# Seven sub-products for eight in one feed-forward layer of a two-layer diffusion backbone

## What is computed

```
def swiglu(t, w_in, w_out):
    gate, up = jnp.split(t @ w_in, 2, axis=-1)
    return (jax.nn.silu(gate) * up) @ w_out
h = h + 0.5 * m[:, 2] * swiglu(modulate(h, m[:, 0], m[:, 1]), w_ff1_in[l], w_ff1_out[l])
```

## Time and profile before

| | |
|---|---|
| median of three runs | 3309.25 us |
| span of the profiled execution | 3311.0 us (its own time is not given apart from the span) |
| TensorE busy | 3172.9 us, 96% |
| VectorE busy | 1640.3 us, 50% |
| ScalarE busy | 964.7 us, 29% |
| third feed-forward with its seam | about 2059 to 2625 us |
| its TensorE clock | 0.99 of 2.4 GHz |

### The profile page before, as it was taken

One profiled execution on the slowest core, in us unless ns is written; L12 is line 12 of the kernel. 1 busy time (PEld: TensorE's weight loads), 2 busy tenths in 40 slices (PEclk: granted clock), 3 DMA queues, 4 the chain that ended last, 5 costly groups with the idle time before them and its releaser, 6 DMA issues.

```text
span 3311.0 us, 44353 instructions
## 1 busy us (share of the span) xinstructions
PE 3172.9 (96%) x18215; PEld 2864.7 (87%) x18215; DVE 1640.3 (50%) x2387; ACT 964.7 (29%) x1470; POOL 264.1 (8%) x316
## 2 busy tenths in 40 slices
PE   5999999999999999899999999999999998999999
PEld 4999999976669894489999999999999976678887
DVE  7754536434542736847634355432236547743333
ACT  4211212355441321233212122211212346632222
POOL 1100000200000006610000001000000100000000
PEclk8999999999999999999999999999999999999999
DMA  6533424411004220014423242322224120023332
GB/s 207 171 102 111 118 72 133 134 28 53 1 1 134 64 64 1 1 51 134 146 71 95 69 136 76 96 83 64 64 72 142 54 64 14 4 87 95 96 99 92
DMA packets 381726, 272.90 MB, mean 82 GB/s; under 512 B 17411, under 2 KB 357626, under 8 KB 381434
## 3 DMA queue, kind: packets, MB, share of 16 engines
q1 hardware_dynamic: 354576, 182.35, 19.0%
q0 software_dynamic: 25344, 88.09, 8.5%
q10 hardware_dynamic: 1641, 0.14, 0.0%
HBM read 262.16 MB, written 8.39 MB: 82 GB/s over the span
## 4 chain that ended last, share of the span: by engine, by line
PE 54%; ACT 2%; DVE 2%; issue 1%; POOL 0%; ACTq 0%; DVEq 0%
PE ps L464 48%; PE ps L1402 1%; ACT gpt L1441 1%; PE ps L1426 1%; PE ps L1384 1%; PE ps L1160 1%; DVE u_lo L612 1%; DVE hid_f L600 1%; ACT gp L1454 1%; PE ps L1841 0%; PE ps L1858 0%; PE ps L1842 0%; PE ps L1848 0%; PE ps L1875 0%; PE ps L698 0%
## 5 line engine op out<-in xcount | busy, mean ns | idle before, releaser
L464 PE MATMUL ps<-u_hi,w_hi 128*128 128x384 f32 (+2 forms) x2992 | 827.7, 346 | 24.3 <-DVE u_lo L612 19.1
L464 PE MATMUL ps<-u_lo,w_hi 128*128 128x384 f32 (+2 forms) x2992 | 820.7, 344 | 0.0
L464 PE MATMUL ps<-u_hi,w_lo 128*128 128x384 f32 (+2 forms) x2992 | 820.1, 343 | 0.0
L454 DVE TENSOR_TENSOR w_lo<-ring,w_hi 128x1024 fp32r<-128x1024 f32 (+3 forms) x357 | 413.4, 1159 | 788.1 <-ACT w_hi L439 593.8
L464 PEld LDWEIGHTS ps<-u_hi,w_hi 128*128 128x128 f32 x2992 | 539.4, 189 | 55.3 <-issue 27.7
L464 PEld LDWEIGHTS ps<-u_lo,w_hi 128*128 128x128 f32 x2992 | 541.6, 189 | 22.0 <-issue 1.7
L464 PEld LDWEIGHTS ps<-u_hi,w_lo 128*128 128x128 f32 x2992 | 541.1, 189 | 20.8
L439 ACT CAST w_hi<-ring 128x1024 fp32r<-128x1024 f32 (+3 forms) x229 | 221.6, 968 | 976.1 <-PE ps L464 940.2
L464 PE MATMUL ps<-hid_hi,w_hi 128*128 128x384 f32 (+1 forms) x1232 | 340.3, 345 | 0.0
L464 PE MATMUL ps<-hid_lo,w_hi 128*128 128x384 f32 (+1 forms) x1232 | 339.6, 345 | 0.0
L464 PE MATMUL ps<-hid_hi,w_lo 128*128 128x384 f32 (+1 forms) x1232 | 339.6, 345 | 0.0
(11 more groups left out here) (277 smaller groups left out, 3345.1 us busy)
## 6 DMA issues: line engine op xcount, KB each, us to landing
ring<-in_w_ff_in SPq DMA_DIRECT2D x176, 512.0 KB, 3.8
m_in<-in_w_mod POOLq DMA_DIRECT2D x128, 512.0 KB, 4.0
ring<-in_w_ff_out SPq DMA_DIRECT2D x64, 512.0 KB, 4.1
ring<-in_w_in_e SPq DMA_DIRECT2D x26, 512.0 KB, 3.9
ring<-in_w_ff_out SPq DMA_DIRECT2D x32, 384.0 KB, 3.5
m_first<-in_w_mod POOLq DMA_DIRECT2D x16, 512.0 KB, 13.9
ring<-in_w_out_e SPq DMA_DIRECT2D x16, 512.0 KB, 4.0
ring<-in_w_in_o SPq DMA_DIRECT2D x12, 512.0 KB, 3.8
```

The source lines that it names most:

```text
L454: dve.tensor_tensor(w_lo[:, b:b + WIDE[n]], ring[:, s:s + WIDE[n]], w_hi[:, b:b + WIDE[n]], ALU.subtract).then_inc(w_split_lo, 1)
L464: mm = pe.matmul(ps_at(p, c0, c1) if halved else pair(p)[:, c0:c1], w, x[:, c0:c1], start=start and i == 0, stop=stop and i == 2)
```

## The change

Gate and up of two hidden blocks are taken together, as a 2 x 2 block product: the weights are cut into upper and lower half of the inputs (4 blocks each) and gate and up (256 columns each), the input into the same halves and the first and last 384 tokens. Instead of eight half-size products seven are made, of sums and differences of the blocks. One "body" makes two hidden blocks in seven chunks; a chunk is 24 products of 384 columns (2 output blocks x 4 input blocks x 3 for the precision). Eleven bodies take the place of 22 rounds, in six parts (SPART) of 4, 4, 4, 4, 4 and 2 hidden blocks, each followed by four output chunks of two output blocks each.

The seven inputs (o = 0 to 6) are built at the start, from `u32` (the modulated input in fp32, 8 blocks): chunks 0 and 1 take blocks as they are, for 2 to 6 `dve_s_mix` makes four differences in place on 4 x 384 = 1536 columns, `act_s_high` casts and `dve_s_low` subtracts. The weights come as four blocks of 512 KB per body (R11, R21, R12, R22 in ring slots 0 to 3, rows of 1 KB); VectorE makes three further sums in place and one in a buffer of its own (`dve_s_sum`), and each chunk's weight is split into one of three buffer pairs. PSUM: chunks 0, 3, 4 and 6 pile up in one pair of banks, and ScalarE takes snapshots of it after 0, 3 and 4; chunks 1, 2 and 5 are added to the snapshots by VectorE. The modulation pieces move into the region of the constants (fetched back at the end), 1 to 3 per chunk, and all three jobs are finished at the start of a chunk in the stream. The seam behind has no modulation job left. Several semaphores of the mixers are merged, to have enough of them.

```
-            for i_f in (1, 2):
-                pe_norm(pe, FF_NORM[i_f])
-                pe_ff(pe, i_f)
+            pe_norm(pe, 2)
+            pe_ff(pe, 1)
+            pe_norm(pe, 3)
+            pe_s_ff(pe, 2)
             pe_norm(pe, 4)
+            pe.wait_ge(const_back, 16)
```

The loads, and when they may start (S_OLD is 201, the number of transfers of the layers before):

```
+        def sync_s(f, i_f):
...
+                if ch[0] == "A" and ch[2] == 0:
+                    todo = [(r, w[:, 4 * (r // 2):4 * (r // 2) + 4,
+                                  (r % 2) * FFN + 2 * P * ch[1]:(r % 2) * FFN + 2 * P * ch[1] + 2 * P], 4) for r in range(4)]
...
+                    if free[r] is None:
+                        last = [x for x in range(S_OLD[i_f]) if x % RING == r]
+                        if last:
+                            sp.wait_ge(w_used, last[-1] + 1)
...
+                    else:
+                        sp.wait_ge(c_lo, S_C0[i_f] + free[r] + 1)
+                        if r == 0 and S_ORDER[i_f][free[r]][0] == "A":
+                            sp.wait_ge(s_sum, 4 * (S_B0[i_f] + S_ORDER[i_f][free[r]][1]) + 4)
```

The seam ahead, on ScalarE and VectorE (`act_s_split(.., 0)` waits for the load of R11, `act_s_split(.., 1)` for R12, the third one issued):

```
+        def act_norm_s(act, n, i_f):
+            for c in range(2):
+                act_s_split(act, i_f, c)
+                if n:
+                    act_square(act, n, DB - 2 + c)
...
+            for d in range(DB):
+                act_s_shift(act, n, d, t)
+                act_s_high(act, i_f, d // 4, d % 4)
+        def dve_norm_s(dve, n, i_f):
...
+            for q in range(DB + 1):
...
+                if q:
+                    dve_s_low(dve, i_f, (q - 1) // 4, (q - 1) % 4)
+            if n in MODS_AT:
...
+            dve_s_mix(dve, i_f, 2)
+            dve_s_sum(dve, i_f, 0, 1)
```

(* only in the first body; modulation pieces stand at the end of VectorE's chunks, not in the first body, one at o = 2, two at o = 3, one at o = 4.) At a part's end prod(e 1, 0), the cast and the remainder of the last two hidden blocks stand at the head of the next chunk; an output chunk has split, residual 2q - 1, up to three modulation pieces and residual 2q on VectorE. TensorE waits, per chunk and output block e:

```
+            bank_of = {0: B_A, 1: B_B, 2: B_C, 3: B_A, 4: B_A, 5: B_C, 6: B_A}[o]
+            def bank_ready(e):
+                if o == 0 and b:
+                    pe.wait_ge(z_prod, 4 * (g - 1) + 2 + 2 * e)
...
+                elif o == 3:
+                    pe.wait_ge(z_snap, 6 * g + 1 + e)
+                elif o == 4:
+                    pe.wait_ge(z_snap, 6 * g + 3 + e)
+                elif o == 5:
+                    pe.wait_ge(z_add, 6 * g + 3 + e)
+                elif o == 6:
+                    pe.wait_ge(z_snap, 6 * g + 5 + e)
```

More of the change, by code:

```diff
@@ L398, in ff_names @@
         def ff_names(i_f):
-            return [x for part in PARTS for x in (("ffi", i_f, part), ("out", R_FF(i_f, part)))]
+            return [x for part in PARTS for x in (("ffi", i_f, part), ("out", R_FF(i_f, part)))] if i_f not in STR else []
         transfers = []
@@ L477, in bmod @@
             return v[:, g % 3 * 24:g % 3 * 24 + 24].rearrange("p (q d) -> p q d", q=3)
+        GATE_BY = {g: 1.0 if g % 3 == 1 else -0.5 if FFN_OF[g] in STR else 0.5 for g in range(6)}
         NORM_T = [T, T, T, T, T, SEQ]
@@ new lines, in build @@
+        S_PART0 = [sum(SPART[:p]) // 2 for p in range(len(SPART))]
+        S_PART = [p for p, size in enumerate(SPART) for _ in range(size // 2)]
+        S_OLD = {i_f: BASE[{0: "even", 1: ("ffi", 2, 0), 2: "odd", 3: ("ffi", 3, 0)}[i_f]] if i_f < 3 and not (i_f == 1 and 2 in STR)
+                 else (n_ if i_f == 3 else BASE["odd"]) for i_f in STR}
+        RAW = {0: 0, 2: 1, 1: 2, 3: 3}
+        raw = [ring[:, SLOT * x:SLOT * x + SLOT] for x in range(4)]
+        R11, R21, R12, R22 = raw
+        B_A, B_B, B_C = (4, 5), (0, 2), (1, 3)
@@ new lines, in build @@
+        S_MODS = {}
+        for i_f in STR:
+            jobs = [x for key in sorted(MODS) if key[0] == i_f for x in MODS[key]]
+            todo = []
+            for x in jobs:
+                first = n_first + DB * (JOB[x] - 2)
+                todo += [("p", x, k, first + k, s) for k in range(DB) for s in range(2)] + [("f", x)]
+            plan, c = {}, 0
+            busy = -1
+            for c, ch in enumerate(S_ORDER[i_f]):
+                cap = {2: 1, 3: 2, 4: 1}.get(ch[2], 0) if ch[0] == "A" else 3
+                if ch[0] == "A" and ch[1] == 0:
+                    cap = 0
+                plan[c] = {"dve": [], "pe": []}
+                if busy >= 0 and c == busy + 2:
+                    plan[c]["pe"].append(done)
+                if busy >= 0 and c == busy + 3:
+                    plan[c]["dve"].append(("d", done))
+                    busy = -1
+                while cap > 0 and todo and busy < 0:
+                    x = todo.pop(0)
+                    plan[c]["dve"].append(x)
+                    cap -= 1
+                    if x[0] == "f":
+                        busy, done = c, x[1]
+            assert not todo and busy < 0, (i_f, len(todo), busy)
+            S_MODS[i_f] = plan
@@ new lines, in s_src, with s_loads @@
+        def s_src(ch):
+            if ch[0] == "O":
+                return raw[ch[2]][:, 0:2 * P * SPART[ch[1]]]
+            return {0: R11, 1: R12, 2: esum[:, :], 3: R11, 4: R21, 5: R12, 6: R22}[ch[2]]
+        def s_loads(i_f):
+            n, out = [0] * 4, {}
+            for x in STR:
+                for c, ch in enumerate(S_ORDER[x]):
+                    if ch[0] == "A" and ch[2] == 0:
+                        for r in range(4):
+                            n[r] += 1
+                            out[x, ch[1], r] = n[r]
+                    elif ch[0] == "O":
+                        n[ch[2]] += 1
+                        out[x, "O", ch[1], ch[2]] = n[ch[2]]
+            return out
@@ new lines, in dve_s_split, with dve_s_sum @@
+        def dve_s_split(dve, i_f, c):
+            dve.wait_ge(c_hi, S_C0[i_f] + c + 1)
+            src = s_src(S_ORDER[i_f][c])
+            n = src.shape[-1]
+            dve.tensor_tensor(v_lo_w[c % 3][:, 0:n], src, v_hi_w[c % 3][:, 0:n], ALU.subtract).then_inc(c_lo, 1)
+        def dve_s_sum(dve, i_f, b, k):
+            g = 4 * (S_B0[i_f] + b)
+            if k == 1:
+                for r in (1, 3):
+                    dve.wait_ge(r_full[r], 16 * S_LOAD[i_f, b, r])
+                dve.tensor_tensor(esum[:, :], R21, R22, ALU.add).then_inc(s_sum, 1)
+                return
+            dve.wait_ge(s_sum, g + min(k - 1, 2))
+            if k == 2:
+                dve.wait_ge(c_lo, S_C0[i_f] + S_IDX[i_f]["A", b, 0] + 1)
+                dve.tensor_tensor(R11, esum[:, :], R11, ALU.add).then_inc(s_sum, 1)
+            elif k == 3:
+                dve.tensor_tensor(R21, R11, R22, ALU.subtract).then_inc(s_sum, 1)
+            else:
+                dve.wait_ge(c_lo, S_C0[i_f] + S_IDX[i_f]["A", b, 1] + 1)
+                dve.tensor_tensor(R12, R11, R12, ALU.add).then_inc(s_sum, 1)
```

599 lines of the change are left out of this document (534 added, 65 removed).

## The result

Over 20 runs of each the changed kernel takes 3312.62 us (3308.4 to 3316.85) where the kernel before takes 3308.16 (3304.97 to 3312.73): ratio 1.0013, 95% interval 1.0007 to 1.0019. That is 4.5 us slower, where I had forecast 3.0 faster: a small difference, but both ends of the interval lie above 1.

The account below looks back on a forecast made before the run. The stage was taken as bound by TensorE's number of products. -45.8 + 27.9 + 5.5 + 1.3 + 7.3 + 0.8 = -3.0 us gave 3306.3 us, own range 3300 to 3311, whole range 3292 to 3318.

Parts of the forecast that it names:

- Products: Input side of the third feed-forward: 1848 products instead of 2112, at 0.1733 us each, -45.8 us.
- Seam ahead: Before the stage: weight loads wait for the last product, first product +6.7 us, at 16.0 us after it.
- First body: First seven chunks: VectorE and ScalarE prepare inputs one after the other, 54.0 us for 29.1 of products, 24.9 lost.
- Output products: Output side of the stage: 512+256 columns instead of 384+384, still 0.174 us each, no cost.
- Parts: Six part ends: waits for the last hidden block, +5.5 us; output chunks +0.5, a last-part residual +0.5.
- Steady bodies: Bodies after the first: TensorE waits for nobody, 0 us (0.3 taken).
- Jobs: Three modulation jobs in TensorE's stream instead of one, 2 x 3.65 = +7.3 us (4 if the clock holds).
- the seam behind: After the stage: GpSimd's last accumulation and first sum outlast the last square, +1.1 less 0.3 for modulations, +0.8 us.
- VectorE late in every body: Rival at the add ahead of chunk 5: one microsecond in ten bodies, +10 us, 3316 us; chance 0.12.
- Low clock staying in the first body: Rival: chunks 5 and 6 also run at 0.32 us a product, +9 us, 3315 us; chance 0.10.
- Shorter start: Rival at the stage's start: loads cost 2 us instead of 6.7, first body loses 20, 3293 us; chance 0.30.
- The table load: ScalarE before SiLU in the first body's chunk 4: 1.28 us; at the skill's 2.66, 1.4 us later.

Follow-up runs that it names:

- load_slots: Changed kernel with the first four weight blocks in ring slots 1, 3, 2, 0 and loaded R11, R12, R21, R22 for the first body; 3305.58 us, ratio to before 0.9988.
- sum_on_pe: Changed kernel with GpSimd adding only squares 0 to 4 behind the stage and TensorE adding blocks 5 to 7; 3310.45 us, ratio to before 1.0007.
- mod_seam: Changed kernel with the last modulation job's products moved out of the stream, behind the sums after the stage; 3309.57 us, ratio to before 1.0011.
- last_part4: Changed kernel with parts ordered 4, 4, 4, 4, 2, 4 and separate places for the squares and their sum; 3313.33 us, ratio to before 1.0015.
- merge_only: Kernel before with nothing but the change's merged semaphores; 3308.32 us, ratio to before 1.0001.
- best: Changed kernel with new slots and load order, reordered first-body queues, squares shared with TensorE, last modulation job behind the stage; 3293.21 and 3294.2 us.
- first_body: Changed kernel with sum R21+R22 and its split made early, and snapshots and adds put earlier in the first body's queues; 3308.82 us, ratio to before 1.0001.
- all_four: Changed kernel with ring slots, first-body order, parts 4 4 4 4 2 4 and last modulation job moved, together; 3301.19 us, ratio to before 0.9973.
- rep_after: Changed kernel run again without edits, for a second trace and ratio; ratio to before 1.0016.

## Why the prediction was wrong

- **The stage** was forecast at 562.9 us and came out at 562.65 to 563.69. That the sum fits is luck: errors of +2.8 (seam ahead), -1.4 (first body), 2 to 3 (output products) and -4.8 us (jobs) cancelled. Term by term:
  - *Products* (-45.8): as said.
  - *Seam ahead* (first product at 16.0): 18.8. R12 was in ScalarE's hands 7.4 us after the last product (2062.76) where I had 6.7. Above all the sums ran at the low clock, four in 2.93 us instead of 1.45, which I had not priced, so the second ones began at 10.8 where I had 9.1 and took 2.58 themselves, 1.0 more than before. `load_slots` confirms the cause, the slot of the last transfer: with it both the late load and the low clock in the sums are gone.
  - *First body* (24.9 lost): 23.5, chunk by chunk within 1.5 us of the list.
  - *Output products* (said to cost nothing): wrong by 2.1 to 3.3 us. In the first trace six of them take 1.06 us nearly everywhere, where six of the old shape take 1.04; in the second and third trace 40% and 24% of the stretches of six take 1.04 with the same code. The projection stage of the trace before has both as well, mostly 1.04, and the four pairs of the earlier trace rows were too short a stretch to see the second value.
  - *Parts* (+5.5, though its own terms, 0.7 x 5 and 2.2, make 5.7, and 1.3): about 7, as what is left over; TensorE's waits there (0.47 five times, 1.68 and 0.43) are 5.2 of it.
  - *Steady bodies* (0): no wait in any of ten.
  - *Jobs* (+7.3 for two more, 3.65 each): three at 2.04 without a low clock in the three traces of this kernel, 6.1 us or 2.5 more than the one before.
- **The step that failed is the seam behind, "+0.8".** The first product of the mixer comes 4.0 to 6.3 us later than before, and seam and mixer together are 3.3 to 7.7 us longer over the traces (310.64 to 313.43 against 305.69 to 307.34). I had counted the last accumulation only, as one add behind one square: +1.1, less 0.3 that the traces don't show (5.5 us from the last sum to the first product in both kernels). What the runs showed in its place: the last add starts 0.9 us late, because GpSimd was 1.3 behind at the fourth block and adds 2.0 apart make up little of it while blocks come every 2.1, and it takes 2.6 us instead of 1.83 beside VectorE's split of the next weights (1.85 and 1.22 again in `sum_on_pe`, which keeps the two apart); with this the late sums cost 2.5 us, as `mod_seam` shows where its sums ran at the full clock. In the three traces of the changed kernel the sums ran at the low clock on top of that (1.5 to 2.7 us), and once a second add was long (1.2). `last_part4` and `sum_on_pe` each took GpSimd's late add away in their own way and the first product came at 9.25 and 10.75.
- **The base.** I took the difference between stages off one execution that was itself slow by some 4 us. Every run whose trace and time are both known took 1.8 us longer than its span, so this one took about 3312.8, not the 3311.0 that I compared with the median. Its trace has the low clock twice where `merge_only` does not, behind the job at 2216 and in the mixer at 2722. `merge_only` itself took 3308.9 us, near the median. Against it the stage gained only 0.7 to 1.7 us, not 3. What lies behind the stage is 5.0 to 7.7 us longer against it, which gives +3.3 to +6.0 trace by trace, and 4.5 was measured. I had noted that the median stood below the trace and moved it along; the right question was which waits and clock levels of the trace the median doesn't have.
- **The rivals.** VectorE late in every body: not so. Low clock staying in the first body: not so; chunks 2 and 4 begin with 17 and 14 slow products behind their long waits (6.8 us a chunk instead of 4.2) and recover within the chunk, as expected, and 5 and 6 run at the full clock. Shorter start: not so. None of the rivals had its place behind the stage, so the way in which the kernel became slower was none of mine. The time lies within the range of 3292 to 3318, but outside the forecast's own, 3300 to 3311.
- The table load behaved as the trace of before had it: 1.28 us (at 2098.16), and SiLU started 3.4 us behind it, when VectorE's add was done, so the load delayed nothing.
- Not settled: the end behind the last product is 9.47 us before and 10.0 in most kernels with the change, 9.5 in `sum_on_pe` and `best`. No run was made for it.

## What to carry to other kernels

When an edit makes the pieces behind it shorter, go through every engine that handles one item per piece and compare its time per item with the new interval, at the stage's end above all: GpSimd, busy for 8% of the kernel, was what TensorE waited for there. Look at the last items one by one, since a mean hides the one that counts. Load what is needed first into the buffer that comes free first, and order the in-order queues of a cold start by what TensorE waits for: these two took 9.4 and 4 us off the start, where the change without them had left the stage within 3 us of its old length. Take the base of a forecast from an execution near the median, or say which events of the trace the median lacks.

## What the hardware showed

- GpSimd's add of two 128x768 tensors takes 1.83 to 1.88 us and VectorE's 128x1024 subtraction in SBUF 1.21 to 1.23 where they do not meet. Where they overlap, the rows read as if they took turns. In the first trace of the changed kernel an add runs from 2617.11 to 2618.94; the subtraction that starts beside it at 2617.22 takes 2.80 us and ends 1.08 after that add, and the next add, started at 2619.08, takes 2.60 and ends 1.66 after that subtraction. In the third trace the subtraction starts first (2619.44, the add 2619.52): it takes its 1.21 us, and the add 2.80. VectorE's residuals, which read PSUM, kept 1.14 for two pieces beside the adds.
- The granted clock's falls behind a lull of some 2 us (tiny products, a short wait) are not fixed by the code. Of the changed kernel's nine jobs in three traces none was followed by one, in `load_slots` two of three, in `first_body` one of three, in `all_four` one of two; the wait of 1.68 us at the part of two was followed by one in `rep_after`, `last_part4` and `sum_on_pe`, and not in the other traces. Each costs about 1.5 us (some eleven products 0.32 apart instead of 0.17). The sums behind a wait of 3.5 us ran at the low clock in four traces and, with the same wait, at the full one in `mod_seam`.
- The time of a run goes with its mean granted clock: of 29 runs of the kernel before in one set, the five with 0.986 took 3302.5 to 3304.3 us and the two with 0.982 took 3310.9 and 3312.7. That fits such falls as the source of much of the 10 us over which runs of one kernel scatter; no run shows it singly.
- Six products in turns of 512 and 256 columns take 1.04 us in some stretches and 1.06 in others, in one trace and with one code. What decides between them stays open.
